# Attention stage of a hybrid encoder block: side jobs placed anew, the score queries' row in two copies, and scores and value products interleaved by column half

## Chip, cores and metric

One core of a Trainium2 chip. The metric is the device time of one execution in microseconds (us); lower is better. Engines are called as in the profile: PE (TensorE), PEld (its weight loads), DVE (VectorE), ACT (ScalarE), POOL (GpSimd), SP (the queue that issues DMAs).

## What is computed

One encoder block over 1024 tokens and 16 meta tokens in front, width 1024, float32:

```
hn = rmsnorm(h);  x_lru, g_lru, c_q, c_kv, k_pe = split(hn @ w_in)
y_lru = rg_lru_bidir(dwconv(x_lru)) * gelu(g_lru)
q, k = rmsnorm + rope of 8 heads x 96;  v = 8 heads x 64
y_mla = softmax(q k^T / sqrt(96)) v            (dense, all 1040 positions)
h = h + [rmsnorm(y_lru) || rmsnorm(y_mla)] @ w_out
h = h + (silu(dwconv(gate)) * up) @ w_ffn_down (gate, up = rmsnorm(h) @ w_ffn_up)
```

## The kernel before, in words

Each float32 product is made of three matmuls of values split in a high part and a low part (high x high, high x low, low x high). The front stage projects x, runs the LRU recurrence and makes q, k and v. `attention_out_phase` (line 1024) does attention and the output projection. The FFN follows.

Attention runs over `steps`, pairs (h, s), which are called slots here: heads h from -1 to 8, and nine tiles s of keys (eight of 128 and one of 16). The global number of a slot is g = 9 h + s. In slot g TensorE makes the scores of tile g (two column halves of 512 queries, three matmuls each, `scores`, line 2029) and the products with v of tile g - 2 (again two halves, `pv`). Around them lie four places for side jobs (`place_job`, line 2021), numbered 0 to 3: before, the order of a slot is scores half 0, place 0, scores half 1, place 1, pv half 0, place 2, pv half 1, place 3 (line 2067 on).

Side jobs prepare the next head: `tq0`, `tq1`, `tk0`, `tk1` transpose q and k of that head (ACT writes the high part, DVE the low part), `tm` does its meta tokens, `a0` to `a15` and `am` make rough scores whose maximum DVE takes, and `r` turns the maxima into a row that SP's queue copies into the 97th row of q_h, which scores half 0 of the next head's slot 0 awaits (`row_in`). `x0`, `x1`, `x2` make scores of two meta queries, which ACT copies to `x_one` and a DMA collects in `x_all`; `ys` sums squares of the LRU output. `PREPARE`, `FIRST`, `OWN`, `LRU_SUMS` and `LAST_AHEAD` (lines 1076 to 1086) say in which slot and place each job lies. Head 0 is prepared in slots (-1, s), before any score, where PE has only side jobs and the `WARM` matmuls of the identity that follow some of them. Side jobs use PSUM banks in turn (`side_of`, line 1118); a job waits until the one that last used its bank was read.

For each tile ACT makes two exps of the 128x1024 scores (e_f at L1558, e_h at L1565) once both halves are there (`s_done`); for the 16-key tile three. DVE subtracts them to e_l in two halves (L1748; for the small tile once, e_meta, L1744). pv waits for e_h and e_l of its tile; pv of tile 0 of a head also waits until the accumulator of the head before was copied to o_sb (`o_read`, L1733, in the DVE's slot 1). After a head, SP moves its sums through `recip_row` (line 1165) and DVE multiplies (L1779, y_mla).

ACT works through a slot as: jobs of places 0 and 1, exps, jobs of places 2 and 3, `out_jobs`. DVE: place 0, low half 0 of tile g - 1, places 1 and 2, low half 1, place 3. In the last head, PE places carry the products of the LRU output with w_out (`lru_products`, tiles 0 to 3, 12 matmuls each, in slots 3, 4, 6, 7); tiles 4 to 7 follow after the last pv.

```
for c in range(2):
    if 0 <= g < G: scores(g, c)
    place_job(h, s, js, c)
for c in range(2):
    if 0 <= g - 2 < G: pv(g - 2, c)
    place_job(h, s, js, 2 + c)
```

Of the kernel before, what the change touches and what calls it, by code (L numbers as in the profile page):

```python
# [1023 lines left out]
def attention_out_phase(nc, place, con, qk, v, yl, ym, res_t, x_h, x_l, up_raw, s_h, s_l, halo, bank, dram, sem):  # L1024
# [28 lines left out]
    x_one = place("x_one", M_ATT + 2 * T, (T,))[QK:QK + 2]  # L1053
# [26 lines left out]
    LAST_AHEAD.update({4: ("a5", "x0", "a6", "a7"), 5: ("a8", "x1", "a9", "a10"), 6: ("a11", "x2", "a12", "a13")})  # L1080
# [8 lines left out]
    def side_jobs(h, s):  # L1089

        places = [None] * 4
        ahead = FIRST if h < 0 else LAST_AHEAD if h == END - 1 else PREPARE
        for plan, head in [(ahead, h + 1), (META_QUERIES, h), (LRU_SUMS, h), (OWN, h)]:
            if plan is OWN and not 1 <= h < END:
                continue
            if 0 <= head < HEADS and not (plan is META_QUERIES and h != END) and not (plan is LRU_SUMS and h != END - 2):
# [9 lines left out]
    first = len([j for s in range(SLOTS) for j in side_jobs(-1, s) if j])  # L1106
    BY_ACT = {"r", "x0", "x1", "x2"}
    LOWS = [("tq0", 0), ("tq1", 0), ("tk0", 0), ("tk1", 0)]
# [9 lines left out]
    def side_of(j):  # L1118

        n = number[j]  # L1120
        if n >= first - 3 and n < first:
            return bank(4 + (n - first + 3) % 2, 1)
        return bank([6, 7, 2, 3, 0, 1][n % 6] if n < first else 6 + (n - first) % 2, 1)

    def before(j):

        n = number[j]
        if n < first - 3:
            return jobs[n - 6:n - 5] if n >= 6 else []
        if n < first:  # L1130
            return jobs[n - 2:n - 1] if n == first - 1 else []
        return jobs[n - 2:n - 1] if n > first + 1 else [("r", 0), ("am", 0)]

    def hi_upto(j):

        return sum(HIGH.get(i[0], 0) for i in jobs[:number[j]])
# [133 lines left out]
    L_SLOT = {3: 0, 4: 1, 6: 2, 7: 3}  # L1270
# [46 lines left out]
    def sync(sp):  # L1317
        for h in range(HEADS):

            if h == END:  # L1320
                sp.wait_ge(sem["ysum"], 4)
                for k in range(4):
                    sp.dma_start(raw_of(k), dram["w_out"][P * k:P * k + P, 0:half]).then_inc(sem["wo_a"][k], 16)
            def last_queries():
                wait_read(sp, ("x2", h))
                sp.dma_start(x_all[2 * h:2 * h + 2], x_one).then_inc(sem["x_in"], 16)

            if h == END:
# [4 lines left out]
            if h != END:  # L1333
                last_queries()
# [86 lines left out]
    def scalar(act):  # L1421
        def job(j):
            kind, h = j
            b = h % 2
            side = side_of(j)
            if kind in HIGH or kind in BY_ACT:
                act.wait_ge(sem["side_done"], number[j] + 1)
# [28 lines left out]
            elif kind[0] == "x":  # L1456
                c = int(kind[1])
                w = 512 if c < 2 else META
                if c == 0:
                    if h:  # L1460
                        act.wait_ge(sem["x_in"], 16 * h)
                    else:
                        act.wait_ge(sem["rope_done"], NT)
                nc.scalar.activation(x_one[:, 512 * c:512 * c + w], side[0:2, 0:w], ACT.Copy)\
# [25 lines left out]
        def std_y(w):  # L1490
            act.wait_ge(sem["y_var"], 2 * w + 1)
            if w == 0:
                wait_read(act, ("ys", END - 2))
# [3 lines left out]
        def out_jobs(h, s):  # L1497
# [7 lines left out]
            if (h, s) == (END - 2, 2):  # L1505
                act.wait_ge(sem["side_done"], number[("ys", END - 2)] + 1)
# [24 lines left out]
        for h, s in steps:  # L1531
# [8 lines left out]
            if h == HEADS and s == 2:  # L1540
                read_output(h)
# [32 lines left out]
        split_y("L", 6)  # L1574
        split_y("L", 7)
# [35 lines left out]
    def vector(dve):  # L1611
# [48 lines left out]
        def out_jobs(h, s):  # L1660
# [15 lines left out]
            if (h, s) == (HEADS, 1):  # L1676
                split_w(4)
                split_w(5)
                add_lru(4)

        def job(j):
# [3 lines left out]
            if kind in HIGH:  # L1685
# [6 lines left out]
            if kind[:2] in ("tq", "tk"):  # L1692
                cs = slice(512 * int(kind[2]), 512 * int(kind[2]) + 512)
                hi, lo = (q_h[b], q_l[b]) if kind[1] == "q" else (k_h[b], k_l[b])
                if j == ("tq0", 0):
                    dve.wait_ge(sem["rope_done"], NT)
                ins = low(lo[:, cs], side[0:QK], gain[kind[1]], hi[0:QK, cs])
# [37 lines left out]
        for h, s in steps:  # L1735
# [33 lines left out]
            if h >= 1 and s == (4 if h < HEADS else 2):  # L1769
                dve.wait_ge(sem["sums_in"], 16 * h)  # L1770
                nc.vector.reciprocal(rs, rs).then_inc(sem["sums_recip"], 1)
                if h == HEADS:
                    split_w(6)
                    split_w(7)
                    add_lru(5)
                    add_lru(6)
            if h >= 1 and s == (7 if h < HEADS else 2):
                dve.wait_ge(sem["recip_in"], 16 * h)
                nc.vector.tensor_tensor(y_of(h - 1), rb, o_sb[0:VD], ALU.mult).then_inc(sem["y_mul"], 1)  # L1779
            if h == HEADS - 1 and s == 1:  # L1780
# [117 lines left out]
    def tensor(pe):  # L1898
        WARM = {"tk0": 10, "am": 8}
        WARM.update({f"a{n}": 1 for n in range(2 * XT)})  # L1900
# [4 lines left out]
        def job(j):  # L1905
# [5 lines left out]
            if number[j] < 6 or j == ("tm", 0):  # L1911
                done = {"tq0": 8, "tq1": 8, "tk0": 8, "tk1": 8}.get(kind, NT)
                pe.wait_ge(sem["q_scaled"], done)
                pe.wait_ge(sem["kv_read"], done)
                pe.wait_ge(sem["rope_done"], done)
                pe.wait_ge(sem["v_full"], done)
# [14 lines left out]
            elif kind[0] == "a":  # L1931

                pe.wait_ge(sem["side_hi"], hi_upto(j))
# [3 lines left out]
            elif kind == "ys":  # L1937
                pe.wait_ge(sem["ysum"], 3)
                ins = sums_y(0, side)
# [26 lines left out]
            if h == 0 and kind in WARM:  # L1966
                if kind == "a0":
                    pe.wait_ge(sem["kv_read"], NT)
                for _ in range(WARM[kind]):
                    nc.tensor.matmul(bank(3 if kind == "tk0" else 5)[:, 0:P], ident, ident, start=True, stop=True)  # L1970
# [24 lines left out]
        def sums_y(w, ps):  # L1995

            for j in range(NT):
# [23 lines left out]
        def place_job(h, s, js, i):  # L2021
            if js[i]:
                job(js[i])
            elif h == END and (s, i) in X_TILES:
                meta_pv(s, i)
            if h == END and s in L_SLOT:
                lru_products(L_SLOT[s], i)

        def scores(g, c):
# [13 lines left out]
            if c == 1:  # L2043
                ins.then_inc(sem["s_done"], 1)

# [21 lines left out]
        for h, s in steps:  # L2067
            if (h, s) == (0, 0):
                pe.wait_ge(sem["b_set"], 2)
            js = side_jobs(h, s)  # L2070
            g = SLOTS * h + s
            for c in range(2):
                if 0 <= g < G:
                    scores(g, c)
                place_job(h, s, js, c)
            for c in range(2):
                if 0 <= g - 2 < G:
                    pv(g - 2, c)
                place_job(h, s, js, 2 + c)

        for j in range(4, XT):
# [1070 lines left out]
```

## Time and profile before

| what | us |
|---|---|
| median of 3 runs (lowest, highest) | 1299.45 (1298.88, 1300.28) |
| the profiled execution, its own time | 1303.02 |
| span of its records | 1301.2 |
| mean granted TensorE clock in it | 0.993 of full speed |

The profiled execution took 1.8 us around its span and is 3.57 us above the median. Times in a trace count from the span's start. A PE matmul of 512 columns is shown with some 0.39 us, but the next starts earlier; the pace is read from starts.

### The profile page before, as it was taken

What the parts mean: (1) busy time and instruction counts of PE and PEld (TensorE: products, weight loads), DVE (VectorE), ACT (ScalarE), POOL (GpSimd) and SP (SyncE); (2) the same over time, 40 slices, a digit from 0 to 9 for tenths busy, and PEclk for the clock granted to TensorE, in tenths of its full rate; (3) what the DMA queues carried; (4) which work ended last, traced back from release to release, by engine and by line L of the source; (5) the groups of instructions that cost most, each with busy time, mean ns of one, the idle gap of its engine ahead of it and who ended that gap; (6) DMA issues with size and microseconds to landing.
All of it is one profiled execution on the core that took longest, in us unless ns stands there. A gap on an engine that the chain in (4) does not pass through costs nothing.

```text
span 1301.2 us, 18506 instructions
## 1 busy us (share of the span) xinstructions
PE 1271.2 (98%) x6158; PEld 1018.6 (78%) x6158; DVE 996.9 (77%) x1505; ACT 769.3 (59%) x1156; POOL 146.6 (11%) x175
## 2 busy tenths in 40 slices
PE   7999999899999999999999999999999999999998
PEld 7999997666666666687678888888888888888886
DVE  6677569678887876577779887887878887887855
ACT  7487648567765866534445565656474565656460
POOL 3000037400000001322200000000010000000010
PEclk9999999999999999999999999999999999999999
DMA  6111200000000014200144846576574847576667
GB/s 220 34 53 41 74 1 1 1 1 10 9 9 10 9 58 155 69 30 1 49 148 94 187 100 166 118 169 134 151 169 93 189 97 169 113 170 133 157 143 245
DMA packets 40938, 123.01 MB, mean 95 GB/s; under 512 B 7378, under 2 KB 8082, under 8 KB 34484
## 3 DMA queue, kind: packets, MB, share of 16 engines
q0 software_dynamic: 7200, 52.43, 21.4%
q1 hardware_dynamic: 33684, 69.86, 15.7%
q8 instruction: 33, 0.54, 0.2%
q14 instruction: 21, 0.17, 0.0%
HBM read 62.34 MB, written 59.80 MB: 94 GB/s over the span
## 4 chain that ended last, share of the span: by engine, by line
PE 85%; DVE 6%; ACT 5%; issue 2%; DMA 1%; POOL 0%; SPq 0%; DVEq 0%; ACTq 0%
PE banks L2911 30%; PE banks L2983 14%; PE banks L100 7%; PE banks L102 7%; PE banks L101 7%; PE banks L1935 2%; PE banks L2040 2%; PE banks L2041 2%; PE banks L2042 2%; PE banks L2060 2%; PE banks L2063 2%; PE banks L2061 2%; ACT e_f L1558 1%; PE banks L1895 1%; ACT e_h L1565 1%
## 5 line engine op out<-in xcount | busy, mean ns | idle before, releaser
L2911 PE MATMUL banks<-x_hi,slot_h 128*128 128x512 f32 x616 | 242.8, 394 | 2.5 <-DVE slot_l L2599 1.3
L2911 PE MATMUL banks<-x_lo,slot_h 128*128 128x512 f32 x616 | 243.4, 395 | 0.0
L2911 PE MATMUL banks<-x_hi,slot_l 128*128 128x512 f32 x616 | 242.9, 394 | 0.0
L2384 ACT ACTIVATE slot_h<-up_raw 128x512 fp32r<-128x512 f32 x127 | 79.8, 629 | 174.4 <-PE banks L2911 172.3
L2911 PEld LDWEIGHTS banks<-x_hi,slot_h 128*128 128x128 f32 x616 | 115.6, 188 | 30.9 <-DVE slot_l L2599 2.1
L2911 PEld LDWEIGHTS banks<-x_lo,slot_h 128*128 128x128 f32 x616 | 115.7, 188 | 27.1
L2911 PEld LDWEIGHTS banks<-x_hi,slot_l 128*128 128x128 f32 x616 | 115.7, 188 | 26.9
L2462 ACT ACTIVATE staged<-banks 128x1024 f32<-128x1024 f32 x100 | 101.4, 1026 | 41.0 <-PE banks L2983 41.0
L2983 PE MATMUL banks<-dn_h,a_h 128*128 128x512 f32 x280 | 110.4, 394 | 0.0
L2983 PE MATMUL banks<-dn_h,a_l 128*128 128x512 f32 x280 | 109.5, 391 | 0.0
L2983 PE MATMUL banks<-dn_l,a_h 128*128 128x512 f32 x280 | 109.5, 391 | 0.0
L1558 ACT ACTIVATE e_f<-banks 128x1024 f32<-128x1024 f32 (+1 forms) x72 | 73.5, 1021 | 60.5 <-PE banks L2042 60.2
L2367 POOL DMA_DIRECT2D down_sums<-staged x50 | 44.1, 881 | 570.5 <-ACT staged L2462 495.6
L100 PE MATMUL banks<-xn_h,win_h 128*128 128x346 f32 (+5 forms) x304 | 96.4, 317 | 1.5 <-DVE xn_l L669 1.5
L1703 DVE TENSOR_REDUCE lam_t<-banks 128x1 f32<-128x512 f32 x128 | 86.2, 686 | 13.8 <-PE banks L1935 13.7
L102 PE MATMUL banks<-xn_h,win_l 128*128 128x346 f32 (+5 forms) x304 | 95.2, 313 | 0.0
L101 PE MATMUL banks<-xn_l,win_h 128*128 128x346 f32 (+5 forms) x304 | 95.1, 313 | 0.0
L2599 DVE TENSOR_TENSOR slot_l<-up_raw,slot_h 128x512 fp32r<-128x512 f32 x127 | 86.8, 685 | 3.2 <-ACT slot_h L2384 3.2
L1748 DVE TENSOR_TENSOR e_l<-e_f,e_h 128x512 fp32r<-128x512 f32 x128 | 87.0, 690 | 1.5 <-ACT e_h L1565 1.4
L2742 DVE SCALAR_TENSOR_TENSOR gate_conv<-gate,par,gate_conv 128x1024 f32<-128x1024 f32 x44 | 55.6, 1283 | 24.7 <-ACT gate_conv L2476 20.3
L1565 ACT ACTIVATE e_h<-banks 128x1024 fp32r<-128x1024 f32 x64 | 65.2, 1019 | 0.0
L2690 DVE TENSOR_TENSOR dn_l<-dn_raw,dn_h 128x512 fp32r<-128x512 f32 x70 | 48.0, 686 | 18.0 <-ACT dn_h L2448 17.9
(346 smaller groups left out, 2861.5 us busy)
## 6 DMA issues: line engine op xcount, KB each, us to landing
down_sums<-staged POOLq DMA_DIRECT2D x50, 1024.0 KB, 8.0
up_raw<-in_w_up SPq DMA_DIRECT2D x88, 256.0 KB, 3.3
dn_raw<-in_w_down SPq DMA_DIRECT2D x22, 512.0 KB, 6.6
win_raw<-in_w_in SPq DMA_DIRECT2D x11, 512.0 KB, 3.3
x_tm<-in_x_tm SPq DMA_DIRECT2D x8, 512.0 KB, 6.0
wo_raw<-in_w_out SPq DMA_DIRECT2D x16, 256.0 KB, 4.1
h<-in_x_tm SPq DMA_DIRECT2D x8, 512.0 KB, 5.7
down_sums<-h SPq DMA_DIRECT2D x3, 1024.0 KB, 6.6
```

The lines of the kernel that those rows point to most:

```text
L100: nc.tensor.matmul(out, w_h, x_h, start=first, stop=False)
L101: nc.tensor.matmul(out, w_h, x_l, start=False, stop=False)
L102: return nc.tensor.matmul(out, w_l, x_h, start=False, stop=last)
L1558: nc.scalar.activation(e_f[g % 3][0:n], s_ps(g)[0:n], ACT.Exp, scale=SCALE)
L1565: ins = nc.scalar.activation(e_h[g % 3], s_ps(g), ACT.Exp, scale=SCALE)
L1703: ins = nc.vector.tensor_reduce(mx3[:, i:i + 1], side, AX.X, ALU.max)
L1748: nc.vector.tensor_tensor(e_l[(g - 1) % 2][:, cs], e_f[(g - 1) % 3][:, cs], f32(e_h[(g - 1) % 3][:, cs]), ALU.subtract).then_inc(sem["e_lo ...
L2384: nc.scalar.activation(s_h[slot], x, ACT.Copy).then_inc(sem["up_hi"], 1)
L2462: nc.scalar.activation(staged[b][:, 2 * p:2 * p + 2, :], bank(4 + 2 * p, 2).rearrange("p (i n) -> p i n", i=2), ACT.Copy).then_inc(sem["dn ...
L2599: nc.vector.tensor_tensor(s_l[slot], x, f32(s_h[slot]), ALU.subtract).then_inc(sem["up_lo"], 1)
L2911: ins = nc.tensor.matmul(o, s[slot][:, k], xs[w], start=fresh and k == 0 and n == 0, stop=k == 3 and n == 2, skip_group_check=not fresh)
L2983: ins = nc.tensor.matmul(bank(4 + i), x[:, ts], w, start=k in FRESH and n == 0, stop=n == 2, skip_group_check=k not in FRESH)
```

## The change

It edits only `attention_out_phase`:

1. Order of a slot: scores half 0, place 0, pv half 0, place 1, scores half 1, place 2, pv half 1, place 3. The jobs' place numbers keep their order in time.
2. Head 0 is prepared in six slots instead of eight, in the order tq0, tk0, tq1, tk1, over all eight PSUM banks; a0 to a3 need only the first halves of q and k. The identity matmuls come ahead of a job instead of behind it, in other numbers. The meta queries of head 0 move into its own slots.
3. `scores_ahead`: the scores of tiles 0 and 1 of head 0 are made over 96 rows before the row of maxima is there, and four matmuls of one row each add it afterwards. `keep_busy` puts eight identity matmuls into slots 0 and 1 of head 0. The high parts of tq0 and tq1 of head 1 are made by DVE.
4. `x_one` is held twice; x0, x1, x2 of heads 1 to 6 move from slots 1, 1, 2 to slots 1, 2, 4, those of head 7 from (6, 4), (6, 5), (6, 6) to (6, 5), (6, 6), (6, 8). SP's copy of `x_one` is issued behind `recip_row`; for the last head it stays ahead of the row of maxima.
5. `ys` moves from one place of slot (5, 1) to the four places of slot (4, 8).
6. The LRU products of tile 4 (`L_GAP`) are made ahead of the last pv; ACT and DVE take the last splits and adds in a new order. SP loads w_out's first blocks at head 6's turn, behind `recip_row`.

```
-    FIRST = dict(PREPARE)
-    FIRST.update({8: ("x0", "x1", "x2", "")})
-    OWN = {1: ("", "", "x0", "x1"), 2: ("", "x2", "", "")}
+    LAST_AHEAD.update({5: ("a8", "x0", "a9", "a10"), 6: ("a11", "x1", "a12", "a13"), 8: ("x2", "", "", "")})
+    FIRST = {0: ("tq0", "tk0", "tq1", "tk1"), 1: ("a0", "a1", "a2", "a3"), 2: ("a4", "a5", "a6", "a7"),
+             3: ("tm", "a8", "a9", "a10"), 4: ("a11", "a12", "a13", "a14"), 5: ("a15", "am", "r", "")}
+    OWN = {1: ("", "", "x0", ""), 2: ("", "x1", "", ""), 4: ("", "x2", "", "")}
+    SECOND = dict(PREPARE)
+    SECOND.update({0: ("", "", "tq0", "tq1"), 1: ("", "", "", "tk0")})
+    OWN_FIRST = {2: ("", "x0", "", ""), 4: ("", "x1", "", ""), 5: ("", "x2", "", "")}
-    LRU_SUMS = {1: ("ys", "", "", "")}
+    LRU_SUMS = {8: ("", "", "", "ys")}
+    YS_TILES = ((0, 1, 2), (3, 4), (5, 6), (7, 8))
...
+    SPLIT_BY_DVE = [("tq0", 1), ("tq1", 1)]
+    FIRST_KEYS = [("a0", 0), ("a1", 0), ("a2", 0), ("a3", 0)]
...
     def sync(sp):
-            if h == END:
-                sp.wait_ge(sem["ysum"], 4)
-                for k in range(4):
-                    sp.dma_start(raw_of(k), dram["w_out"][P * k:P * k + P, 0:half]).then_inc(sem["wo_a"][k], 16)
             def last_queries():
                 wait_read(sp, ("x2", h))
-                sp.dma_start(x_all[2 * h:2 * h + 2], x_one).then_inc(sem["x_in"], 16)
+                if h:
+                    sp.wait_ge(sem["x_in"], 16 * h)
+                sp.dma_start(x_all[2 * h:2 * h + 2], x_one[h % 2]).then_inc(sem["x_in"], 16)
...
             if h:
                 recip_row(sp, h - 1)
+            if h == END - 1:
+                sp.wait_ge(sem["ysum"], 4)
+                for k in range(4):
+                    sp.dma_start(raw_of(k), dram["w_out"][P * k:P * k + P, 0:half]).then_inc(sem["wo_a"][k], 16)
+            if h != END:
+                last_queries()
...
     def scalar(act):
             if h == HEADS and s == 2:
+                split_y("L", 6)
                 read_output(h)
...
     def vector(dve):
             if (h, s) == (HEADS, 1):
+                add_lru(L_GAP)
                 split_w(4)
                 split_w(5)
-                add_lru(4)
...
     def tensor(pe):
-        WARM = {"tk0": 10, "am": 8}
-        WARM.update({f"a{n}": 1 for n in range(2 * XT)})
+        WARM = {"tq0": 2, "tk0": 2, "tq1": 4, "tk1": 2, "a0": 6, "r": 2}
+        WARM.update({f"a{n}": 2 for n in range(2, 2 * XT)})
+        HEAD_0 = {"tq0": (8, 4, 4, 0), "tk0": (8, 4, 4, 0), "a0": (NT, 0, 0, 0), "a1": (NT, 0, 0, 0),
+                  "tq1": (8, 8, 8, 0), "tk1": (8, 8, 8, 0)}
...
+        def scores_ahead():
+            pe.wait_ge(sem["b_set"], 2 + len(LOWS))
+            for g in range(2):
+                ks = slice(P * g, P * g + P)
+                for c in range(2):
+                    cs = slice(512 * c, 512 * c + 512)
+                    out = s_ps(g)[:, cs]
+                    nc.tensor.matmul(out, k_h[0][0:QK, ks], q_h[0][0:QK, cs], start=True, stop=False)
+                    nc.tensor.matmul(out, k_h[0][0:QK, ks], q_l[0][:, cs], start=False, stop=False)
+                    nc.tensor.matmul(out, k_l[0][:, ks], q_h[0][0:QK, cs], start=False, stop=False)
+            pe.wait_ge(sem["row_in"], 16)
+            for g in range(2):
+                for c in range(2):
+                    cs = slice(512 * c, 512 * c + 512)
+                    ins = nc.tensor.matmul(s_ps(g)[:, cs], k_h[0][QK:QK + 1, P * g:P * g + P], q_h[0][QK:QK + 1, cs],
+                                           start=False, stop=True)
+                ins.then_inc(sem["s_done"], 1)
+        def keep_busy(n):
+            for _ in range(n):
+                nc.tensor.matmul(bank(5)[:, 0:P], ident, ident, start=True, stop=True)
...
         for h, s in steps:
             if (h, s) == (0, 0):
-                pe.wait_ge(sem["b_set"], 2)
+                scores_ahead()
...
             for c in range(2):
-                if 0 <= g < G:
+                if 2 <= g < G:
                     scores(g, c)
-                place_job(h, s, js, c)
-            for c in range(2):
+                place_job(h, s, js, 2 * c)
+                if g - 2 == G - 1 and c == 0:
+                    for k in range(LF):
+                        lru_products(L_GAP, k)
                 if 0 <= g - 2 < G:
                     pv(g - 2, c)
-                place_job(h, s, js, 2 + c)
+                elif 0 <= g < 2:
+                    keep_busy(2)
+                place_job(h, s, js, 2 * c + 1)
```

## Rows read from the trace of the kernel before

**Rows 1.** The page: busy us, share of the span and count by engine
```profile
PE 1271.2 (98%) x6158; PEld 1018.6 (78%) x6158; DVE 996.9 (77%) x1505; ACT 769.3 (59%) x1156; POOL 146.6 (11%) x175
```

**Rows 2.** Busy time by stage: stretch, length, each engine's us (x count), PEclk, DMA, GB/s
```profile
224.90:247.90 23.00, 18.16 (x121) 15.55 (x120) 15.25 (x30) 10.30 (x21) 15.55 (x18) 0.93 0.00 1
...
527.30:551.05 23.75, 21.02 (x90) 14.13 (x88) 13.94 (x18) 14.28 (x24) 6.78 (x8) 0.93 0.24 75
...
640.00:1301.20 661.20, 651.90 (x2851) 528.96 (x2849) 528.45 (x815) 366.43 (x551) 52.77 (x56) 1.00 0.61 146
```

**Rows 3.** Timeline 224 to 248: start, us, engine, line, operation, [idle before, releaser]
```profile
226.29 1.49 PE L1920 MATMUL banks<-ident,qk 128*96 128x128 f32 x12 [1.36 <-POOL qk L416]
...
227.29 1.23 ACT L1433 ACTIVATE q_h<-banks,par 96x512 fp32r<-96x512 f32 x2
...
227.61 2.40 PE L1970 MATMUL banks<-ident 128*128 128x128 f32 x20
...
231.31 0.47 PE L1935 MATMUL banks<-k_h,q_h 96*128 96x512 f32 x1 [0.86 <-ACT k_h L1433]
...
231.82 3.08 DVE L1703 TENSOR_REDUCE lam_t<-banks 128x1 f32<-128x512 f32 x5 [2.51 <-PE banks L1935]
...
235.44 0.47 PE L1935 MATMUL banks<-k_h,q_h 96*128 96x512 f32 x1 [1.40 <-ACT k_h L1445]
...
235.64 2.61 POOL L1381 TENSOR_TENSOR k_l<-qk_full,k_h 96x512 fp32r<-96x512 f32 x2
...
244.81 0.27 PE L1942 MATMUL banks<-ident,lam_t 128*8 128x128 f32 x1
...
245.42 0.81 SPq L1331 DMA_DIRECT2D q_h<-r_row  x1
...
247.94 0.47 PE L2040 MATMUL banks<-q_h,k_h 97*128 97x512 f32 x1 [1.25 <-DMA q_h<-r_row]
```

**Rows 4.** Timeline 532 to 552, end of attention
```profile
532.68 2.30 DVE L1744 TENSOR_TENSOR e_meta<-e_f,e_meta 16x1024 fp32r<-16x1024 f32 x1
...
535.13 0.64 PE L2057 MATMUL banks<-e_meta,v_meta 80*66 80x512 f32 x2 [2.73 <-DVE e_meta L1744]
...
546.49 1.22 DVE L1779 TENSOR_TENSOR y_mla<-sum_recip,o_sb 64x1024 f32<-64x1024 f32 x1
...
551.05 0.39 PE L100 MATMUL banks<-wo_h,y_h 128*128 128x512 f32 x1
```

**Rows 5.** Busy time of two stretches, the second at half the clock
```profile
312.44:324.81 12.37, 11.79 (x61) 7.55 (x60) 9.01 (x12) 11.95 (x16) 0.00 (x0) 1.00 0.01 2
420.57:423.98 3.41, 3.41 (x12) 1.73 (x11) 1.45 (x3) 1.74 (x3) 0.00 (x0) 0.50 0.00 0
```

**Rows 6.** Timeline at 418, PE
```profile
418.18 1.97 PE L1998 MATMUL banks<-ones,y_sum 128*128 128x2 f32 x18
```

**Rows 7.** The chain in order of time, FFN: start, us, what
```profile
671.61 19.78 PE banks L2911 x84
```

**Rows 8.** Timeline 309 to 323, turn from head 1 to head 2, all engines
```profile
309.59 0.48 PE L2040 MATMUL banks<-q_h,k_h 97*16 97x512 f32 x1
...
311.27 1.02 ACT L1558 ACTIVATE e_f<-banks 16x1024 f32<-16x1024 f32 x1 [1.13 <-PE banks L2042]
...
314.24 0.68 ACT L1433 ACTIVATE q_h<-banks,par 96x512 fp32r<-96x512 f32 x1
...
315.73 1.21 DVE L1744 TENSOR_TENSOR e_meta<-e_f,e_meta 16x1024 fp32r<-16x1024 f32 x1
...
317.85 0.48 PE L2057 MATMUL banks<-e_meta,v_meta 80*66 80x512 f32 x1
...
320.14 1.21 DVE L1733 COPY o_sb<-banks 66x1024 f32<-66x1024 f32 x1
...
322.59 0.42 PE L2060 MATMUL banks<-e_h,v 128*66 128x512 f32 x1
```

**Rows 9.** Timeline at 484, the queue of SP
```profile
484.46 0.67 SPq L1331 DMA_DIRECT2D q_h<-r_row  x1
```

More of the change, by code:

```diff
@@ L1051, in attention_out_phase @@
     r_row = place("r_row", at, (P,), F32R, XT); at += P
-    x_one = place("x_one", M_ATT + 2 * T, (T,))[QK:QK + 2]
+    x_one = [place(f"x_one{b}", M_ATT + (2 + b) * T, (T,))[QK:QK + 2] for b in range(2)]
     x_all = place("x_all", M_ATT + 4 * T + 2 * T, (T,))[QK:QK + NX]
@@ L1106, in attention_out_phase @@
     first = len([j for s in range(SLOTS) for j in side_jobs(-1, s) if j])
+    side_banks = [2, 3, 6, 7, 0, 1, 4, 5] + [(6, 7, 4, 5, 2, 3, 0, 1)[n % 8] for n in range(first - 9)] + [4] +\
+                 [6 + n % 2 for n in range(len(jobs) - first)]
     BY_ACT = {"r", "x0", "x1", "x2"}
-    LOWS = [("tq0", 0), ("tq1", 0), ("tk0", 0), ("tk1", 0)]
+    LOWS = [("tq0", 0), ("tk0", 0), ("tq1", 0), ("tk1", 0)]
     full = [place(f"qk_full{n}", WORDS - 8 - 512 * (n + 1), (512,), parts=QK) for n in range(len(LOWS))]
@@ L1118, in side_of @@
     def side_of(j):
[L1120 to L1123, printed above, removed]
+        return bank(side_banks[number[j]], 1)
     def before(j):
         n = number[j]
[L1128 to L1132, printed above, removed]
+        return [i for i in jobs[:n] if side_banks[number[i]] == side_banks[n]][-1:]
+    SPLIT_BY_DVE = [("tq0", 1), ("tq1", 1)]
+    FIRST_KEYS = [("a0", 0), ("a1", 0), ("a2", 0), ("a3", 0)]
     def hi_upto(j):
-        return sum(HIGH.get(i[0], 0) for i in jobs[:number[j]])
+        return 2 if j in FIRST_KEYS else sum(HIGH.get(i[0], 0) for i in jobs[:number[j]] if i not in SPLIT_BY_DVE)
     def wait_read(eng, j):
@@ L1459, in job @@
                 if c == 0:
[L1460 to L1461 removed]
+                    if h >= 2:
+                        act.wait_ge(sem["x_in"], 16 * (h - 1))
                     else:
                         act.wait_ge(sem["rope_done"], NT)
[L1464 removed]
+                nc.scalar.activation(x_one[h % 2][:, 512 * c:512 * c + w], side[0:2, 0:w], ACT.Copy)\
                   .then_inc(sem["side_read_act"], 1)
@@ L1696, in job @@
                     dve.wait_ge(sem["rope_done"], NT)
+                if j in SPLIT_BY_DVE:
+                    link(nc.vector.tensor_scalar(hi[0:QK, cs], side[0:QK], gain[kind[1]], None, ALU.mult))
                 ins = low(lo[:, cs], side[0:QK], gain[kind[1]], hi[0:QK, cs])
@@ L1910, in job @@
                 wait_read(pe, i)
[L1911 to L1916, printed above, removed]
+            if number[j] < 8 or j == ("tm", 0):
+                for name, done in zip(("q_scaled", "kv_read", "rope_done", "v_full"), HEAD_0.get(kind, (NT,) * 4)):
+                    if done:
+                        pe.wait_ge(sem[name], done)
+            if h == 0 and kind in WARM:
+                for _ in range(WARM[kind]):
+                    nc.tensor.matmul(side[:, 0:P], ident, ident, start=True, stop=True)
             if kind[:2] in ("tq", "tk"):
@@ L1965, in job @@
             ins.then_inc(sem["side_done"], 1)
[L1966 to L1970, printed above, removed]
         def meta_pv(s, i):
@@ L1993, in meta_columns, with sums_y @@
             return ins
-        def sums_y(w, ps):
-            for j in range(NT):
+        def sums_y(w, ps, tiles=range(NT)):
+            for j in tiles:
                 ins = nc.tensor.matmul(ps[0:out_rows(j), 2 * j:2 * j + 2], y_sum[:, sum_cols(w, j)], ones[:, 0:2],
@@ L2021, in place_job @@
         def place_job(h, s, js, i):
+            sums = ("ys", END - 3)
             if js[i]:
                 job(js[i])
+            elif (h, s) == (END - 3, XT):
+                if i == 0:
+                    for j in before(sums):
+                        wait_read(pe, j)
+                    pe.wait_ge(sem["ysum"], 3)
+                sums_y(0, side_of(sums), YS_TILES[i])
             elif h == END and (s, i) in X_TILES:
                 meta_pv(s, i)
-            if h == END and s in L_SLOT:
-                lru_products(L_SLOT[s], i)
+            if (h, s) in L_SLOT:
+                lru_products(L_SLOT[h, s], i)
         def scores(g, c):
```

41 lines of the change are left out of this document (23 added, 18 removed).

## Prediction

> **What bounds the kernel now.** The page comes first: PE is busy for 98% of the span [rows 1]. Busy time by stage then says where there is room. After 640 us PE is busy for 651.9 of 661.2 us and nothing is edited there [rows 2]; a gain made earlier is kept whole. Room lies in two stretches: 224.9 to 247.9, the preparation of head 0, with PE busy 18.2 of 23.0, and 527.3 to 551.05, the end of attention, 21.0 of 23.75, both with a granted clock of 0.93 [rows 2]. The timeline shows what PE waits for there. In the first: POOL's rope (1.36), high parts (0.86), the meta tokens' high parts (1.40) and the DMA of the row of maxima (1.25) [rows 3]. In the second: DVE's e_meta (2.73) [rows 4]. A stretch of 3.41 us around 421 stands at the lower level, 1.2 GHz (0.50) [rows 5]; PE had just made sums of two columns [rows 6]. Between lies the steady part: at a head's turn PE stands still little, and ACT is busy for 11.95 of 12.37 us [rows 5]. The order of a slot matters there, for what delays ACT's start delays that whole stretch.
>
> **Prices.** 84 matmuls of 512 columns take 19.78 us, 0.235 each [rows 7]; a column half of scores or of pv (three) 0.70. An identity call is two matmuls, and 20 of these take 2.40, the last one's end included [rows 3]: 0.23 a call. A side job a is 0.235, a transposing job 0.35 to 0.45, x0 or x1 0.70.
>
> **Head 0 prepared.** PE can begin at 224.9, where its idle time of 1.36 began [rows 3], since tq0 and tk0 no longer wait for the last rope. Four transposing jobs (1.8) and ten identity calls (2.3) end at 229.1; six more calls bring a0 to 230.5, not 231.31, and its high parts are there at 228.5, two of ACT's after 227.29 [rows 3]. From a2 on a job with its two calls costs 0.69, more than DVE's reduction (five in 3.08, 0.62) [rows 3], so PE sets the pace: 0.47 and 14 x 0.69, 0.25 for the meta tokens and 1.0 for am end near 242.1. After DVE r stands at 242.8, against 244.81 [rows 3], where it stood behind eight calls. SP issued 0.6 later and the scores began 2.5 after that [rows 3], so now at 245.9 instead of 247.94. The scores of two tiles (12 x 0.235 = 2.8) lie in that wait; POOL has their low parts ready at 238.3 [rows 3].
>
> What follows in head 0: -2.0 (row), -2.8 (those scores), +0.9 for four matmuls of one row. No row shows such a one. It could be 0.06, as for few columns, or 0.40, a whole matmul not overlapped, which is -0.7 to +0.7 in all; I take 0.235, since its 512 columns are those of [rows 7]. +1.8 for eight identity calls, +1.5 for x0 to x2. DVE gets two high parts, which no row shows on DVE; ACT's two took 1.23 [rows 3] and a reduction of as many columns 0.69, so 0.6 to 0.9 each, and I take 0.7. Its chain (two high, two low parts, two halves of e_l, tk0's low part) ends at 252.5, and x0 waits some 0.9 for it; with small ones 1.5 of waits, against 1.9 in these slots now. Sum: **-1.0**.
>
> **The order of a slot.** Take the turn from head 1 to 2 and T = 309.59, the start of slot 8. ACT's first exp of the small tile starts at T+1.68, behind both score halves. With a pv half between them it starts at T+2.38. All that ACT and DVE have queued behind moves by 0.70: q_h (T+4.65) to T+5.35; e_meta (T+6.14) to T+6.84, its end to T+8.05; o_sb (T+10.55) to T+11.25, its end to T+12.46 [rows 8]. PE in turn comes to its pv earlier. Pv of the small tile, at T+8.26 now, stands behind one score half only: slot 1 begins at T+6.4, so T+7.2, a wait of **0.85**. Pv of tile 0, at T+13.0 now [rows 8], comes after tk0, x0, tk1, two score halves and two short pv: 8.1+0.35+0.70+0.35+1.5+0.48 = T+11.45, a wait of **1.0** for o_sb. The same stretch holds some 1.2 of small waits now (0.58 by the busy time [rows 5], which counts the matmuls' ends), and these go, as x0, x1 and x2 stand further apart. Net +0.6, and 0.05 for tm's low parts behind later exps. From slot 5 on ACT catches up. Heads 1 to 4: **+2.6**. Heads 5 and 6 lack ACT's square at the turn: +0.35 each, before what follows.
>
> The row of a later head: exps of slot 7 end 0.94 later, where ACT had been idle before r, so r_row goes 0.1 later, and there is that much slack. Nothing. DVE's halves of e_l wait for later exps, covered by a slot of slack; without that cover each slot would cost up to 0.7. The copy of x_one behind recip_row costs nothing: the second copy covers it until two heads later.
>
> **Head 5 and the sums.** The sums (18 matmuls, 1.97 [rows 6]) only move, but stand in small groups between full matmuls. 3.41 us at half the clock do 1.7 us of work; I take 1.6 as the cost, and that it goes. Slot 8 becomes 1.9 longer, so e_meta is on time but o_sb is not: +0.85 over now. **-0.75**. Head 6: +0.35, less 0.35 of a wait behind w_out's load, which ACT meets later: **0**.
>
> **The row of the last head.** SP now waits for x2 in slot (6, 8) before it may issue the row, which it issued at 484.46, 0.6 into that slot [rows 9]. ACT comes to x2 behind r and a split of w_out, 1.3 into it; the copy takes 0.15, SP's issue of x_all 0.65. The row landed within 2.5 of its issue [rows 3]; here, with the issue itself 0.67 instead of 0.81, I take 2.0: 4.1, where PE is ready at 2.85. Queued behind it on SP are loads of x only. **+1.2** (0.9 to 1.7). In slots 2 to 4 of head 7 the wait for o_sb grows by 0.45 and that of the second LRU product shrinks by 0.55: **-0.1**.
>
> **The end.** Before the last pv PE stood 2.73 us; then came half clock. Now 12 matmuls (2.8) lie there, whose inputs are ready. The three exps of slot (7, 8) end 0.70 later and so does e_meta, with its 2.30 [rows 4] (1.21 in [rows 8]; POOL subtracts beside it): a wait of 0.7 stays. That gains 2.2, and 1.6 for the clock: 3.7. Next late is y_mla: DVE's multiply, at 546.49 now [rows 4], no longer stands behind an add and comes 1.7 earlier; PE would be at the next product 3.7 before 551.05 [rows 4] and waits 0.6 for it. **-3.0**.
>
> **Sum:** -1.0+2.6-0.75+0+1.2-0.1-3.0 = -1.05 us. Against the profiled execution's own 1303.02 that is 1301.97; it lies 3.57 above the median, so 1299.45 becomes **1298.4**. Under 0.2% (2.6 us) a measurement of this kernel can't tell from no change.
>
> **Rivals.**
> (1) The two waits at a head's turn don't come: ACT's chain has slack that I miss. Then heads 1 to 6 cost nothing more: -2.6-0.85-0.35, 1294.6, a little less if the small waits go as well. For it: two jobs leave the crowded stretch. Against: ACT, e_meta and o_sb follow each other closely in the rows. 0.25.
> (2) The clock falls in the new places too, in head 0's preparation and at the sums, where it falls now: 1298.4+1.6+1.6 = 1301.6. Against: the wait of 1.40 that stood before the first goes. 0.15.
> (3) Slower: the waits of 0.85 and 1.0 at each head's turn bring the clock down. A fall costs up to 1.7 by the stretch at 0.50; in six heads 1298.4+9.6 = 1308, and it decides from the third head on (1303.2). Against: 2.73 us of waiting, and 1.40 with 0.86, stood before falls, but single waits of under 1 us didn't bring one. 0.10. By the Trainium skill ("TensorE: Matmul & The Clock Gate", the section on a second failure mode with PSUM queues) short idle times between groups of matmuls, come often enough, make the clock swing; by that page this rival would be the likelier one. The trace has the clock at 1.00 over the turns of heads 1 to 4, so I leave it at its chance.
> (4) The lag adds up: DVE reads the side banks late in every head, at the price of the 0.70 once more: six times, 1302.6. 0.12.
> (5) The row isn't hidden: a wait in slots (-1, s) (banks, POOL's subtractions) stands in its place, 1299.4 to 1300.5. 0.05.
> The forecast has 0.33. Faster: (1) and a third of the forecast, 0.36. Slower: (3) and (4), 0.22. Same: the rest, 0.42. The range leaves out (3) and the tips of (1) and (4): 1293.5 to 1302.5; the forecast's own is 1296.5 to 1300.5.
>
> **What would show it.** Right: r near 242.8 and PE on scores until the row lands; e_meta and o_sb as what PE waits for in slots 1 and 2 of heads 1 to 6 (neither now), 34.4 us a head instead of 33.8; about 1.2 us of waiting for the row before head 7; under 1 us before the last pv; full clock around 421 and 537. Wrong: 33.8 a head or less, rows of 0.50 within heads, or a row that doesn't come earlier.

## The result, and the profile after

The changed kernel takes **1307.1 us** (median of 4 runs, 1306.25 to 1307.54), the kernel before beside it 1299.16 (1296.82 to 1300.28): a ratio of **1.0062**, 95% interval 1.0048 to 1.0076. It is 7.9 us slower, where 1298.4 was predicted and the range ended at 1302.5. The profiled execution of the changed kernel took 1307.46 us for a span of 1305.4, so it lies 0.36 above its median; the one of before lay 3.9 above its own (1303.02 against 1299.16). Span against span the change costs only 4.2 us; why the two differences part is said further down.

The page and the busy time by stage, which answer to [rows 1, 2]:

```profile
PE 1273.1 (98%) x6202; PEld 1020.7 (78%) x6202; DVE 998.1 (76%) x1507; ACT 768.0 (59%) x1154; POOL 147.6 (11%) x175
```

```profile
224.90:247.90 23.00, 22.87 (x161) 19.90 (x159) 16.14 (x30) 10.34 (x20) 16.06 (x19) 1.00 0.00 1
...
535.36:555.98 20.62, 19.60 (x90) 12.80 (x88) 12.30 (x17) 13.11 (x22) 6.43 (x7) 1.00 0.29 92
644.50:1305.40 660.90, 652.48 (x2852) 529.38 (x2852) 528.73 (x815) 366.64 (x552) 53.26 (x57) 1.00 0.61 146
```

The holes of [rows 2] are filled as meant: PE is busy for 22.87 of 23.00 us where it was for 18.16, and for 19.60 of 20.62 from slot 8 of the last head to the first product of the out-projection. The clock shows 1.00 in both, and from 15.3 to 1305.5 us it never leaves 2.4 GHz in this execution. The stretch behind attention is as long as in this profile of before. The time must have been lost between, and busy time by slot finds it. First the turn to head 2 in the kernel before, then in the changed one; columns as in [rows 2], the stretches are slots 0 to 4 of head 2:

```profile
312.44:316.01 3.57, 3.57 (x22) 2.62 (x20) 1.02 (x2) 3.53 (x5) 0.00 (x0) 1.00 0.02 5
316.01:320.37 4.36, 3.95 (x22) 2.31 (x20) 3.78 (x6) 4.36 (x6) 0.00 (x0) 1.00 0.00 0
320.37:324.81 4.44, 4.28 (x23) 2.62 (x22) 4.20 (x6) 4.06 (x7) 0.00 (x0) 1.00 0.01 2
324.81:328.59 3.78, 3.78 (x19) 2.50 (x17) 3.78 (x7) 2.04 (x3) 0.00 (x0) 1.00 0.02 1
328.59:332.14 3.55, 3.55 (x18) 2.58 (x17) 2.88 (x7) 2.08 (x4) 0.00 (x0) 1.00 0.00 0
```

```profile
314.01:317.60 3.59, 3.59 (x22) 2.67 (x20) 0.40 (x1) 3.55 (x5) 0.00 (x0) 1.00 0.00 0
317.60:321.67 4.07, 3.28 (x19) 2.07 (x17) 3.46 (x5) 4.07 (x6) 0.00 (x0) 1.00 0.00 0
321.67:327.01 5.34, 4.55 (x23) 2.97 (x22) 5.06 (x8) 4.07 (x7) 0.00 (x0) 1.00 0.01 1
327.01:330.80 3.79, 3.79 (x19) 2.50 (x17) 3.79 (x7) 1.99 (x4) 0.00 (x0) 1.00 0.00 0
330.80:335.23 4.43, 4.01 (x21) 2.61 (x20) 2.90 (x7) 2.38 (x7) 0.00 (x0) 1.00 0.00 0
```

Slots 1 and 2 (the second and third line) together take 9.41 us for 8.80: the +0.6 that was predicted. **Slot 4 takes 4.43 for 3.55**, where almost nothing was. A head takes 35.3 us (head 2 from slot 8 to slot 8: 311.13 to 346.47), not 34.4, and before 33.8. The timeline of the turn shows the two waits of the prediction in their places:

```profile
313.51 1.02 ACT L1567 ACTIVATE e_f<-banks 16x1024 f32<-16x1024 f32 x1 [1.78 <-PE banks L2062]
...
317.98 1.22 DVE L1757 TENSOR_TENSOR e_meta<-e_f,e_meta 16x1024 fp32r<-16x1024 f32 x1
...
319.34 0.42 PE L2101 MATMUL banks<-e_meta,v_meta 80*66 80x512 f32 x1 [0.79 <-DVE e_meta L1757]
...
322.39 1.21 DVE L1746 COPY o_sb<-banks 66x1024 f32<-66x1024 f32 x1
...
323.75 0.42 PE L2104 MATMUL banks<-e_h,v 128*66 128x512 f32 x1 [0.79 <-DVE o_sb L1746]
```

With T = 311.13, the start of slot 8, e_f starts at T+2.38 and e_meta ends at T+8.07 (predicted T+8.05), o_sb at T+12.47 (T+12.46). Slot 4 of the same head, all engines:

```profile
329.78 1.03 ACT L1567 ACTIVATE e_f<-banks 128x1024 f32<-128x1024 f32 x1 [1.80 <-PE banks L2062]
...
330.70 1.02 ACT L1574 ACTIVATE e_h<-banks 128x1024 fp32r<-128x1024 f32 x1
...
331.37 0.39 PE L2062 MATMUL banks<-q_h,k_l 96*128 96x512 f32 x1
331.61 0.27 ACT L1451 ACTIVATE q_h<-banks,par 96x16 fp32r<-96x16 f32 x1
331.76 0.27 ACT L1453 ACTIVATE k_h<-banks,par 96x16 fp32r<-96x16 f32 x1
...
332.15 0.19 PEld L1954 LDWEIGHTS banks<-k_h,q_h 96*128 96x128 f32 x1 [0.82 <-issue]
332.18 0.47 PE L1954 MATMUL banks<-k_h,q_h 96*128 96x512 f32 x1 [0.42 <-ACT k_h L1453]
```

L1954 is the side job a5. PE would start it 0.23 after 331.37, at 331.60, but it starts at 332.18. It waits for the counter of high parts, which includes tm's two. ACT makes those behind the exps of slot 3, and the first of these starts 2.77 us after the slot does (329.78 against 327.01). In the kernel before it is 1.83 (326.64 against 324.81), since only a job, not a job and a pv half, stands between the two score halves. There k_h's part ends at 329.12, 0.26 before a5 starts:

```profile
326.64 1.03 ACT L1558 ACTIVATE e_f<-banks 128x1024 f32<-128x1024 f32 x1 [1.73 <-PE banks L2042]
...
328.86 0.26 ACT L1445 ACTIVATE k_h<-banks,par 96x16 fp32r<-96x16 f32 x1
...
329.38 0.39 PE L1935 MATMUL banks<-k_h,q_h 96*128 96x512 f32 x1
```

So the exps come 0.94 later, 0.26 of it was slack, and 0.68 is left for PE. The waits by engine and line, 275 to 500 us, say how often it and the two others come (us in total, times, longest):

```profile
PEld banks L2101 <- ACT e_h L1574: 6.0, 5, 1.2
PEld banks L1954 <- issue: 4.9, 6, 0.8
PEld banks L2104 <- ACT e_h L1574: 4.9, 5, 1.0
...
PE banks L2104 <- DVE o_sb L1746: 4.6, 6, 0.9
PE banks L2101 <- DVE e_meta L1757: 3.9, 5, 0.8
...
PE banks L1954 <- ACT k_h L1453: 2.5, 6, 0.4
```

Three waits in nearly every head (the one by "issue" is the weight load in front of the wait for k_h). In the same view of before o_sb comes once, with 0.8 us in head 7, and the other two never. At the end, where [rows 4] had 2.73 us of waiting for e_meta, 0.69 is left, and y_mla is the next that is late:

```profile
541.42 2.33 DVE L1757 TENSOR_TENSOR e_meta<-e_f,e_meta 16x1024 fp32r<-16x1024 f32 x1
...
543.90 0.65 PE L2101 MATMUL banks<-e_meta,v_meta 80*66 80x512 f32 x2 [0.69 <-DVE e_meta L1757]
...
552.75 1.22 DVE L1791 TENSOR_TENSOR y_mla<-sum_recip,o_sb 64x1024 f32<-64x1024 f32 x1 [2.15 <-DMA sum_recip<-recip]
...
555.97 0.50 PE L100 MATMUL banks<-wo_h,y_h 128*128 128x512 f32 x1 [0.33 <-POOL y_l L1399]
```

### The profile page after: what moved, and what is told of

Read it like the earlier page. It is cut to its first block, busy times and chain, and to the rows that moved or that the text cites. A ratio compares the mean times of both kernels' runs of the same rounds, so it can differ in the third digit from the quotient of the medians.

```text
span 1305.4 us, 18581 instructions
## 1 busy us (share of the span) xinstructions
PE 1273.1 (98%) x6202; PEld 1020.7 (78%) x6202; DVE 998.1 (76%) x1507; ACT 768.0 (59%) x1154; POOL 147.6 (11%) x175
## 4 chain that ended last, share of the span: by engine, by line
PE 85%; DVE 7%; ACT 6%; issue 2%; DMA 1%; POOL 0%; SPq 0%; DVEq 0%; ACTq 0%
PE banks L2959 31%; PE banks L3031 15%; PE banks L100 7%; PE banks L102 7%; PE banks L101 7%; PE banks L1954 2%; PE banks L2104 2%; PE banks L2060 2%; PE banks L2061 2%; PE banks L2062 2%; PE banks L2107 2%; PE banks L2105 2%; ACT e_f L1567 2%; ACT e_h L1574 1%; PE banks L1909 1%
## 5 line engine op out<-in xcount | busy, mean ns | idle before, releaser
L1567 ACT ACTIVATE e_f<-banks 128x1024 f32<-128x1024 f32 (+1 forms) x72 | 73.7, 1024 | 74.8 <-PE banks L2062 70.4
```

Source lines behind the costliest of these rows:

```text
L1567: nc.scalar.activation(e_f[g % 3][0:n], s_ps(g)[0:n], ACT.Exp, scale=SCALE)
```

## The experiments

Theory A: the half-by-half order is what costs, through ACT's later start: at e_meta, at o_sb, and at tm's high parts in slot 4. Theory B: the new places of x0 to x2, of the sums, or DVE's high parts cost it. Theory C: half by half costs something in every slot. The question beside it: what are the other parts worth?

**The order put back.** All else of the change stays.

```
             for c in range(2):
                 if 2 <= g < G:
                     scores(g, c)
-                place_job(h, s, js, 2 * c)
+                place_job(h, s, js, c)
+            for c in range(2):
                 ...
-                place_job(h, s, js, 2 * c + 1)
+                place_job(h, s, js, 2 + c)
```

> The changed kernel with the slot's order put back: scores of both halves (a side job behind each), then pv of both halves (a side job behind each). All else of the change stays. Theory A (the order costs it: at each head's turn the waits for e_meta and o_sb, and in slot 4 the wait of a5 for tm's high parts, together 1.5 us a head in heads 1 to 6): heads take 33.8 us again, the waits for e_meta, o_sb and k_h are gone, and the time falls by 8 to 9.5 us, to 1298 or 1299. Theory B (the places of x0 to x2 and of the sums cost it, or DVE's two high parts): the period stays above 35 us and the time stays above 1305. If A holds but the medians show no gain over the kernel before, then the other parts of the change are worth nothing in the median, although they take three falls of the clock out of the profile.

Measured: 1294.66 us (7 runs) beside 1300.73 before; ratio 0.996, interval 0.9945 to 0.9974. More than expected: 12.4 us by the medians, 13.3 by the ratios (the changed kernel was measured beside 1299.16, this one beside 1300.73), and 13.1 by the two traces up to the first out-projection product (555.97 and 542.88). A head takes 33.5 us, 1.8 less than in the changed kernel in heads 1 to 4, where 1.5 was expected. B falls. Slots 1, 2 and 4 of head 2:

```profile
314.25:317.34 3.09, 3.09 (x19) 2.14 (x17) 2.51 (x4) 3.09 (x5) 0.00 (x0) 1.00 0.00 0
317.34:322.72 5.38, 4.84 (x23) 2.80 (x21) 5.38 (x8) 5.07 (x7) 0.00 (x0) 1.00 0.01 1
...
326.50:330.19 3.69, 3.69 (x21) 2.64 (x20) 2.90 (x7) 2.13 (x5) 0.00 (x0) 1.00 0.00 0
```

Slots 1 and 2 take 8.47 us, 0.94 less than in the changed kernel and 0.33 less than before; slot 4, where x2 now stands, takes 3.69, 0.74 less than in the changed kernel and 0.14 more than before. With the old order the other parts gain some 0.3 us a head (33.5 for 33.8), most likely through the new places of x0 to x2; no run has these places alone. PE's waits for e_meta, o_sb and k_h aren't in this trace's view of 275 to 500 us.

**The order alone, in the kernel before.**

> The kernel before with only the order of a slot changed (scores half, job, pv half, job, twice); jobs keep their numbers and their sequence. Theory A: 1.4 to 1.6 us more in each of heads 1 to 6, so +8 to +10 us, 1307 to 1309, with PE waiting for e_meta, o_sb and for ACT's k_h before a5. Theory B: within 2 us of the kernel before.

```
             for c in range(2):
                 if 0 <= g < G:
                     scores(g, c)
-                place_job(h, s, js, c)
-            for c in range(2):
+                place_job(h, s, js, 2 * c)
                 if 0 <= g - 2 < G:
                     pv(g - 2, c)
-                place_job(h, s, js, 2 + c)
+                place_job(h, s, js, 2 * c + 1)
```

Measured: 1310.48 (6 runs) beside 1300.73; 1.0075, 1.0058 to 1.0092, that is +9.8 us. A part of that may be the clock: its profiled execution shows 0.50 at 235.54, for 6.83 us from 426.69, and at 546.16, its six runs had mean granted clocks of 0.992 to 0.997, those of before beside it 0.994 to 0.999, and its two runs at 0.997 took 1306.6 and 1307.3. Heads 1 to 4, with the clock at 1.00, take 35.15 us each, 1.35 more than before. The waits at e_meta and in front of a5 are in its view of waits (275 to 500 us), in each of six heads. o_sb isn't among PE's waits: x0 and x1 both stand in slot 1 here, and PE comes to slot 2 later (head 7's wait for it, 1.65 us, lies behind this view):

```profile
PEld banks L1935 <- issue: 4.9, 6, 0.8
...
PE banks L2057 <- DVE e_meta L1744: 4.2, 6, 0.8
...
PE banks L1935 <- ACT k_h L1445: 2.5, 6, 0.4
```

**The changed kernel without the wait for tm.** a0 to a15 read 1024 keys and 1024 queries, and nothing of the meta tokens.

```
     def hi_upto(j):
 
+        if j[0] in PIECES and j[1]:
+            return sum(HIGH.get(i[0], 0) for i in jobs[:number[j]] if i not in SPLIT_BY_DVE and i != ("tm", j[1]))
         return 2 if j in FIRST_KEYS else ...
```

> The changed kernel, where a0 to a15 of heads 1 to 7 no longer wait for the high parts of the meta tokens (tm), which they don't read; nothing else is edited. Theory A: a5 in slot 4 no longer waits for ACT's k_h, slot 4 falls from 4.4 to 3.7 us, 0.7 to 0.85 a head, and the time falls by 4 to 5 us, to 1302 to 1303. Rival (ACT's lag is what counts: PE only meets ACT a step later, at the exps, the o_sb copy or a wait for e_h): slot 4 shrinks, slots 5 to 8 grow by the same, and the time falls by less than 1 us.

Measured: 1302.58 (12 runs), 4.5 us below 1307.1 (5.2 by the ratios to before); ratio 1.0022, 1.0012 to 1.0033. Slot 4 of head 2:

```profile
329.17:332.95 3.78, 3.78 (x21) 2.66 (x20) 2.81 (x7) 2.38 (x7) 0.00 (x0) 1.00 0.00 0
```

0.65 us less, and slots 5 to 8 don't grow in heads 1 to 4; in head 5 slot 7 takes half of it back (5.03 for 4.70) and in head 6 slot 6 all (5.10 for 4.36; this slot also takes 3.93 to 4.29 in four profiles of before, so a part of that may be chance). From r of head 0 to r of head 6 the traces differ by 3.6 us (211.07 and 207.49). What is left over 3.55 in slot 4 is x2, which stood in slot 2 before.

**The old order in slot 8 alone.**

```
-                place_job(h, s, js, 2 * c)
+                place_job(h, s, js, c if s == XT else 2 * c)
+                if s == XT:
+                    continue
                 ...
+            if s == XT:
+                for c in range(2):
+                    if 0 <= g - 2 < G:
+                        pv(g - 2, c)
+                    place_job(h, s, js, 2 + c)
```

> The changed kernel with the old order in slot 8 of every head alone (both halves of the small tile's scores first, so that ACT starts its exps 0.70 us earlier); slots 0 to 7 keep half by half. Theory A (the lag of ACT that starts at the small tile's scores makes PE wait for e_meta in slot 1; the wait for tm's high parts arises in slot 3 by itself): slot 1 falls by 0.5 to 0.9 us in heads 1 to 6, slot 4 keeps its 4.4 us, the time is 1302.5 to 1304. Theory C (half by half costs in each slot alike, through DVE's and ACT's late start on every tile): nothing in slot 1 changes by more than 0.2, time 1306 to 1307.

Measured: 1303.52 (5 runs) beside 1299.8; 1.0036, 1.0023 to 1.005. Slots 1, 2 and 4 of head 2:

```profile
316.97:320.40 3.43, 3.31 (x19) 1.99 (x17) 2.48 (x4) 3.43 (x6) 0.00 (x0) 1.00 0.00 0
320.40:326.08 5.68, 4.57 (x23) 2.96 (x21) 5.38 (x8) 4.38 (x7) 0.00 (x0) 1.00 0.01 1
329.88:334.31 4.43, 4.01 (x21) 2.61 (x19) 2.89 (x7) 2.38 (x7) 0.00 (x0) 1.00 0.00 0
```

Slot 1 lost 0.64 as theory A says, slot 4 kept its 4.43. But slot 2 took back 0.34 in the wait for o_sb. Up to the last pv the trace is 2.2 us shorter, not the 3.6 of the medians. Behind the out-projection's first product it is 2.1 shorter, where nothing was edited, 1.4 of it after the last matmul; four profiles of before differ by as much there. So 2.2 is what the trace gives to slot 8, and the rest isn't shown to come from it.

**The old order at the turn, half by half elsewhere**, and no wait for tm. The edit is the one above with `s in (8, 0, 1, 2)` and the one on hi_upto.

> The changed kernel with the old order in the four slots of a head's turn (8, 0, 1, 2) and half by half left in slots 3 to 7, and a0 to a15 without the wait for tm's high parts. Theory A (half by half costs in two places alone: the turn, through e_meta and o_sb, and slot 4, through tm): both are removed, so the time is that of the version with the whole old order, 1293.5 to 1296, and slots 3 to 7 take what they take in either order. Theory C (each slot in the half order costs something of its own): 1297 to 1300.

Measured: 1295.22 (6 runs) beside 1300.74; 0.9962, 0.9947 to 0.9976. That is the time of the whole old order. By the time alone C isn't excluded (the interval reaches 1297.6), but the traces do it: heads 1 to 4 take 134.15 us for 134.12. Once a5 is freed of tm, half by half costs less than 0.1 us in any of slots 3 to 7 of these heads; in head 5 slot 7 takes 5.03 us for 4.71.

**The row first.** The order put back, and SP issues the last head's row before it waits for x2.

```
-            if h == END:
-                last_queries()
             wait_read(sp, ("r", h))
             ... the row's dma_start
             if h == END:
+                last_queries()
```

> The changed kernel with the slot's order put back, and SP issues the row of the last head before the transfer that waits for x2. Theory A: PE's wait for the row before head 7 goes, -1.0 us against the version with the order put back alone (1294.7): 1293.7. Rival: PE then meets x2's or the next wait, time unchanged.

Measured: 1294.84 (6 runs) beside 1299.8; 0.9966, 0.9954 to 0.9979; no difference from 1294.66. The rival holds. Slot 8 of head 6 takes 2.95 us for 3.85, and slot 2 of head 7 3.71 for 2.98, because PE is at the next thing that is late:

```profile
487.71 1.21 DVE L1745 COPY o_sb<-banks 66x1024 f32<-66x1024 f32 x1
...
489.07 0.42 PE L2103 MATMUL banks<-e_h,v 128*66 128x512 f32 x1 [0.76 <-DVE o_sb L1745]
```

**The same, without the wait for tm.**

> As the one before it, and a0 to a15 no longer wait for tm's high parts. Theory A (that wait exists only where the half order starts the exps of slot 3 late): no difference from the one before it, within 0.7 us. Rival (a part of the wait is there in either order): 1 to 3 us faster.

Measured: 1293.72 (11 runs), 0.9962, 0.9952 to 0.9972, beside 0.9966 for the one before it: 0.5 us by the ratios, 1.1 by the medians, which is outside the 0.7 stated, but the intervals overlap. A head from slot 8 to slot 8 takes 33.6 us in both, and heads 1 to 4 134.02 in both, so the wait for tm is there only with the half order.

**The end put back.** The order put back, and the LRU product of the gap, its add and its splits where the kernel before has them.

```
-                if g - 2 == G - 1 and c == 0:
-                    for k in range(LF):
-                        lru_products(L_GAP, k)
...
-        for j in range(L_GAP + 1, XT):
+        for j in range(L_GAP, XT):
```

> The changed kernel with the slot's order put back and the LRU products, their adds and their splits of the end back where the kernel before has them (12 matmuls after the last pv instead of ahead of it). By the traces the stretch from the last pv of the small tile to the out-projection took 15.9 us before and 12.1 after: so 3.5 to 4 us slower than 1294.7, 1298.3, and the lower clock level shows again around 532 us. Rival (the end is hidden by something else, as w_out's splits): under 2 us.

Measured: 1299.14 (12 runs); 0.9992, 0.998 to 1.0004. The gap's filling is worth 4.2 us by the ratios, a little more than expected (5.4 by the traces up to the out-projection), and without it the rest of the change, in the old order, is worth nothing that shows. The clock falls again, here for 6.82 us (first line busy time by stretch, then timeline):

```profile
530.49:537.31 6.82, 6.25 (x15) 4.88 (x16) 1.84 (x3) 3.47 (x5) 0.00 (x0) 0.50 0.01 1
```

```profile
531.07 1.09 PE L2099 MATMUL banks<-e_meta,v_meta 80*66 80x512 f32 x2 [2.74 <-DVE e_meta L1756]
```

**The end alone, in the kernel before.**

> The kernel before with one part of the change alone: the 12 matmuls of the LRU product 4 ahead of the last pv, with its add first in DVE's queue and the splits of pieces 6 and 7 earlier in ACT's. Theory A (this part is nearly all that the change gains): 3.5 to 4.8 us faster than the kernel before, and no stretch at the lower clock level around 535 us. Rival (it pays only together with head 0's earlier start and the side jobs' new places): under 2 us.

Measured: 1296.26 (12 runs) beside 1299.3; 0.9971, 0.9958 to 0.9983, so 3.0 us by the medians and 3.8 by the ratio. It pays by itself. No lower level at the end (granted clock 1.00 from 533.57 to 540.40), though this execution had it at 248.04 for 3.41 us and at 422.12 for 6.82.

**The kernel before, profiled again**, three times.

> The kernel before, unchanged, for a second profile. Its first one had three stretches of 3.41 us at the lower clock level inside attention and its own time lay 3.6 us above the median. If those stretches are rare in executions, this profile shows none or one of them and a time of 1299 or 1300; if they belong to the kernel, it shows three again and a time of 1302 to 1304.

> The kernel before once more, unchanged, for a third profile. Theory: the stretch at the lower level at the end of attention (533 to 537 us) is there each time; those at 236 and 421 us come and go, and an execution's time goes with their number: about 1297.4 with the end's alone, 1303 with all three, 1299 to 1301 with one of the two.

> As the one before it: a fourth profile of the kernel before, to see whether its time goes with the number of stretches at the lower level.

Their times were 1297.38, 1300.19 and 1298.16. In each the lower level came once inside attention, at its end, and never at 236 or 421 us. Three stretches of the first of them; the first profile's stretch at 236 showed 0.50, as did [rows 5] at 421:

```profile
533.57:536.98 3.41, 3.41 (x10) 2.64 (x9) 1.41 (x2) 3.20 (x5) 0.00 (x0) 0.50 0.04 6
236.25:239.66 3.41, 3.41 (x25) 3.09 (x24) 3.41 (x6) 0.00 (x0) 3.21 (x4) 1.00 0.02 5
420.57:423.98 3.41, 2.91 (x14) 1.60 (x13) 2.48 (x3) 3.13 (x6) 0.00 (x0) 1.00 0.00 0
```

Of 68 further executions of the kernel before (18, 22, 17 and 11, beside four groups of experiments; 1297.1 to 1305.1 us) three took over 1303 us, and these three alone had a mean granted clock of 0.993, that of the first profile. The profile on which the prediction was made was one of these rare long ones. Single stretches inside heads are less rare: each of the two kernels above with one edit to the kernel before shows one within 12 us of 236 and one within 7 us of 421. None of the eight profiles of the change and its variants has one there. That a time goes with the number of stretches holds only roughly: 1300.19 had the same one inside attention as 1297.38, and in the first 17 us twice as long a stretch at the lower level.

## Why the prediction failed

Against the first profiled execution, by the steps of the prediction. The measured column is the difference of the two traces between the marks named; "the last pv of tile 70" is the last before the wait for e_meta.

| step | predicted | measured | without the wait for tm |
|---|---|---|---|
| up to the end of the front | 0 | +0.4 | +0.2 |
| head 0, to r of head 1 | -1.0 | -0.35 | -1.0 |
| heads 1 to 4, r to r | +2.6 | **+6.0** | +3.4 |
| head 5 | -0.75 | 0.0 | -0.3 |
| head 6 | 0 | +0.8 | +0.9 |
| row of the last head | +1.2 | +1.0 | +1.0 |
| head 7, to the last pv of tile 70 | -0.1 | +0.1 | +0.1 |
| the end, to the out-projection | -3.0 | -3.1 | -3.3 |
| from there on | 0 | -0.7 | -1.2 |
| sum | -1.05 | +4.2 (span) | -0.2 (span) |

**The step that failed is "0.05 for tm's low parts behind later exps".** It asked who waits for the low parts, and left out that a5's counter of high parts includes tm's two. These stand on ACT behind the exps of slot 3, which the half order delays by 0.94; less 0.26 of slack that falls on PE once more a head. In slot 4 the term was mis-sized by 0.62 to 0.67 in each of heads 0 to 6. Heads 5 and 6 give some or all of it back, which leaves 3.6 us by the traces and 4.5 by the medians, most of what separates the first two columns. The prediction had the sign of it in its own rows: the wait of 1.40 that it names "the meta tokens' high parts" is a job a that waits for ACT's k_h of tm [rows 3]. The rule that was applied at slots 8 to 2 (all that ACT has queued behind the exps moves with them: ask who waits for it) was right and wasn't carried to slots 3 and 4. Rival (4) priced a lag that comes once more per head at 1302.6, but named DVE's reading of the side banks; the price was right and the place wrong.

**The second failure is in the last line of the sum.** It took 3.57 us off as the distance between the profiled execution and the median, and had also counted 1.6 for the clock twice, in head 5 and at the end, and a row 2.0 earlier in head 0, all from that one execution. Two of these gains were largely in the median already. From the end of the front to r of head 0 the first profile of before takes 20.3 us and the other three 18.6 to 18.7; the changed kernel takes 18.0, so the usual gain is 0.6, not 2.0. From r to r head 5 takes 37.06 us in the first profile and 36.3 in the others, so the stretch at 421 cost 0.7, not 1.6. That is 2.3 us counted twice. The rest of the distance has nothing to do with the clock inside attention: from the start of the last matmul to the end of the span the first profile takes 6.50 us, the others 4.05, 5.45 and 4.22, and the changed kernel 5.13. So the two profiled times differ by 4.4 us, the medians by 7.9. The stretch at the end comes in all four profiles of before, and its gain is real.

What held: r of head 0 at 243.00 (242.8 predicted), the scores' last rows at 245.99 (245.9), e_meta and o_sb in slots 1 and 2, +0.61 in slots 1 and 2 (+0.6), the row of the last head, 0.69 us before the last pv (0.7), and the end (-3.1 for -3.0; y_mla made PE wait 0.33, not 0.6). In head 7 the wait for o_sb grew by 0.56 (1.31 for 0.75) and that of the second LRU product shrank by 0.47 (0.23 for 0.70), nearly as forecast. In heads 1 to 4 without tm 0.2 a head is still over the forecast, and slot 4 shows it: x2's work moved there. Head 6 is 0.8 over: slots 1 and 2 give 0.49 of it, slot 4 0.11 and slot 6 0.25, where 0.35 less of a wait behind w_out's load was expected. Behind 640 us, where nothing is edited, not all stayed as it was: early in the FFN PE waits for ACT's gate (0.38, before never) and for DVE's slot_l (1.26, before 0.65 to 1.03), which makes 0.6 to 1.0 us more than in the four profiles of before. Why these come later isn't shown.

Rival (1), "the two waits don't come", was priced at 1294.6 us. With the order put back they don't come, and it measured 1294.7. Rivals (2) and (3) fall: the granted clock is 1.00 over all of attention although PE stops for 0.79 us twice and for 0.42 once in nearly every head. By the Trainium skill ("TensorE: Matmul & The Clock Gate", the section on a second failure mode) frequent short idle times between groups of matmuls can make the clock swing; this trace shows no swing at three short waits in 35 us. The kernel before with the order alone has two of the three, and its stretches at 0.50 don't lie at the turns of heads 1 to 4 either. Rival (5) isn't seen: head 0's row is covered.

Where the expected gain went, by the ratios to before: the end -0.3% (-3.8 us alone in the kernel before, -4.2 in the changed one with the old order), the order +0.75% alone, the clock included, and about 1% in the changed kernel (x0 to x2 stand better and PE is earlier there, so that more of the delay shows; that this is the reason is argued, not shown); head 0, the sums, the side jobs' places and the row together nothing that shows (0.9992). **The better version** is the change with the old order: 0.996 (1294.7 us), or 0.9962 (1293.7) with the row first and without the wait for tm; the runs don't tell these two apart, nor clearly from the end alone in the kernel before (0.9971, 0.9958 to 0.9983).

## What to carry to other kernels

When an edit delays one kind of instruction on an in-order engine, walk that engine's whole queue for a full period and look up, for every entry behind it, each counter that it raises and each wait on that counter, also those that ask for more than their operands need. A profiled execution that lies well above the median is not a base from which disturbances may be counted as gains and the distance taken off as well: take a second profile of the kernel before, and count only the stretches that come back. A gap that PE meets with work it has ready pays nearly in full (the 12 matmuls at the end); work that is only brought forward in front of the next late thing pays nothing (the row of the last head).

## What the runs showed beside it

Matmuls of one row by 512 columns (the row of maxima added to scores that are there) took a little longer than full ones:

```profile
245.99 1.19 PE L2081 MATMUL banks<-q_h,k_h 1*128 1x512 f32 x4
```

The last one's end is in the 1.19; with 0.39 for it the others are 0.27 apart, where 0.235 was taken. And executions of the kernel before spread from 1297.1 to 1305.1 us, of which the lower clock level explains the tip only: the granted clock is 0.997 in executions of 1297.36 and of 1301.94 us. The profiles show a part of the rest: the stretch from the last matmul's start to the end of the span takes 4.05 to 6.50 us in the four of before. What else makes it up, and what sets that stretch, stayed open.
